# Two layers of a diffusion backbone with an expert layer: the relay of a unit's chosen experts stands later, diagonals three pairs ahead

## The reference, cut to what matters

```python
s1 = jnp.einsum('thd,kd->thk', q1, sub_k1); s2 = jnp.einsum('thd,kd->thk', q2, sub_k2)
v1, i1 = lax.top_k(s1, 16);  v2, i2 = lax.top_k(s2, 16)
cand_s = v1[..., :, None] + v2[..., None, :];  cand_i = i1[..., :, None] * 128 + i2[..., None, :]
best_s, pos = lax.top_k(cand_s, 16);  idx = take_along_axis(cand_i, pos)
gate = softmax(best_s)
act = gelu(einsum('thkd,td->thk', exp_u[idx], hb))
out = einsum('thk,thkd->td', gate * act, exp_v[idx])
```

## Time and profile before

| | us |
|---|---|
| median of 3 runs | 5514.84 (5513.72 to 5514.99) |
| the profiled execution's own time | 5498.03 |
| its span | 5496.2 |
| busy: PE, DVE, POOL, ACT | 4310.1, 3042.9, 2745.0, 1236.3 |
| PE idle for a unit's `gnorm` at its relay | 163.4, 31 times |
| gathers: bytes, mean rate over the span | 1342 MB, 301 GB/s with the weights |

### The profile page before, as it was taken

One profiled execution on the slowest core, in us unless ns is written; L12 is line 12 of the kernel. 1 busy time (PEld: TensorE's weight loads), 2 busy tenths in 40 slices (PEclk: granted clock), 3 DMA queues, 4 the chain that ended last, 5 costly groups with the idle time before them and its releaser, 6 DMA issues.

```text
span 5496.2 us, 57357 instructions
## 1 busy us (share of the span) xinstructions
PE 4310.1 (78%) x19168; PEld 2423.3 (44%) x19168; DVE 3042.9 (55%) x8176; ACT 1236.3 (22%) x3643; POOL 2745.0 (50%) x2566
## 2 busy tenths in 40 slices
PE   7989788888987878997855558999788799655655
PEld 4468643434675345653411115668534455211111
DVE  1211767786227867457677542521687655776753
ACT  1321222333212321122211113530233111111111
POOL 0000566667205655666677770000366566777776
PEclk8789899988998888998977788999888999777788
DMA  5543799999638978999999992114698899999999
GB/s 194 194 172 133 289 368 356 332 341 352 237 134 298 339 283 327 385 396 368 359 386 382 405 387 80 55 62 150 237 330 317 316 358 396 380 397 389 379 409 349
DMA packets 464130, 1651.73 MB, mean 301 GB/s; under 512 B 51168, under 2 KB 57440, under 8 KB 463840
## 3 DMA queue, kind: packets, MB, share of 16 engines
q0 software_dynamic: 368640, 1342.34, 64.3%
q1 hardware_dynamic: 95200, 305.73, 15.5%
HBM read 1645.77 MB, written 2.10 MB: 300 GB/s over the span
## 4 chain that ended last, share of the span: by engine, by line
PE 43%; POOL 20%; DVE 16%; DMA 10%; issue 8%; ACT 3%; SPq 0%; DVEq 0%; POOLq 0%; ACTq 0%; PEldq 0%
PE banks L653 15%; POOL vb L1457 10%; POOL ub L1446 10%; PE banks L934 8%; DMA vb<-in_peer_v_dram,idx 7%; DVE ub L1397 5%; PE banks L742 4%; PE banks L669 3%; PE banks L844 3%; PE banks L821 3%; PE banks L832 1%; PE banks L782 1%; PE banks L721 1%; PE banks L906 1%; DVE region L1257 1%
## 5 line engine op out<-in xcount | busy, mean ns | idle before, releaser
L1446 POOL DMA_INDIRECT ub<-in_peer_u_dram,idx x1280 | 1394.9, 1090 | 2164.8 <-DVE idx L1385 1330.3
L934 PE MATMUL banks<-vb,dg 128*64 128x512 f32 x5120 | 1565.4, 740 | 693.7 <-DMA vb<-in_peer_v_dram,idx 599.8
L1397 DVE CUSTOM_DVE_ANT_0 ub<-ub,h2cur 128x1024 f32<-128x1024 f32 x1280 | 1529.0, 1222 | 591.1 <-DMA ub<-in_peer_u_dram,idx 470.9
L1457 POOL DMA_INDIRECT vb<-in_peer_v_dram,idx x1280 | 1349.5, 1054 | 569.1 <-issue 356.8
L934 PEld LDWEIGHTS banks<-vb,dg 128*64 128x64 f32 x5120 | 407.8, 160 | 1588.0 <-issue 1351.8
L653 PE MATMUL banks<-region,wring 128*128 128x256 f32 x3840 | 885.7, 390 | 39.6 <-ACT region L998 25.3
L653 PEld LDWEIGHTS banks<-region,wring 128*128 128x128 f32 x3840 | 740.1, 195 | 220.8 <-issue 108.3
L1145 ACT ACTIVATE dg<-consts,wgt 128x64 f32<-128x64 f32 x1280 | 358.9, 338 | 829.8 <-PE banks L934 416.9
L653 PE MATMUL banks<-h2T,wring 128*128 128x256 f32 x1280 | 318.1, 406 | 20.8 <-ACT h2T L998 20.8
L1340 DVE SCALAR_TENSOR_TENSOR region<-region,banks 128x256 f32<-128x256 f32 x120 | 50.5, 421 | 488.5 <-PE banks L653 488.4
L742 PE MATMUL banks<-region,wring 128*128 128x256 f32 (+1 forms) x1056 | 260.7, 406 | 48.0 <-ACT region L998 48.0
(11 more groups left out here) (146 smaller groups left out, 3711.4 us busy)
## 6 DMA issues: line engine op xcount, KB each, us to landing
wring<-w_gate_dram SPq DMA_DIRECT2D x120, 512.0 KB, 4.6
wring<-w_mod_dram SPq DMA_DIRECT2D x96, 512.0 KB, 4.5
wring<-w_pq_dram SPq DMA_DIRECT2D x80, 512.0 KB, 6.0
wring<-w_branch_dram SPq DMA_DIRECT2D x60, 512.0 KB, 4.8
wring<-w_out_dram SPq DMA_DIRECT2D x40, 512.0 KB, 4.2
ub<-in_peer_u_dram,idx POOLq DMA_INDIRECT x1280, 6.9
vb<-in_peer_v_dram,idx POOLq DMA_INDIRECT x1280, 6.9
region<-in_na_rpb_dram SPq DMA_DIRECT2D x64, 256.0 KB, 3.1
```

The costliest lines, as they stand in the source:

```text
L934: ins = nc.tensor.matmul(bank(ACC[a])[64 * g:64 * g + 64, :], dg[:, n % DG_RING, :], vb[:, n % V_RING, a * 512:(a + 1) * 512], start=first ...
L1397: nc.vector.tensor_tensor_reduce(out=ub[:, n % U_RING, :], in0=ub[:, n % U_RING, :], in1=h2cur[:, g, :], scale=1.0, scalar=0.0, op0=ALU.mu ...
L1446: pool.indirect_dma_start(ub[:, n % U_RING, :], None, u_rows, bass.IndirectOffsetOnAxis(ap=idx[:, u % IDX_RING, j:j + 1], axis=0)).then_in ...
L1457: pool.indirect_dma_start(vb[:, n % V_RING, :], None, v_rows, bass.IndirectOffsetOnAxis(ap=idx[:, u % IDX_RING, j:j + 1], axis=0)).then_in ...
```

## The change

Relay and index leave the chain of a unit's choice. The choice now has five steps (`topk` 0 to 3 and `gnorm`), and `bgs["front"]` counts five to a unit. The relay of unit `u` is written behind part 1 of unit `u + 1`, its index behind part 3 of `u + 1`, both in the same background step as that part and without a turn of their own. So each background step still has one step of choice (or two), but five instead of seven make a unit. A unit that no later unit's choice follows has its relay and index written by `chosen(u)`, right ahead of its own first dots, or by `until_front` at the start of a query stage. The number of units that the choice may be ahead is as before. Diagonals stand three pairs ahead of the sum instead of two, `wgt` with them one pair earlier. No computation is added or dropped. The foreground, the dots and the sums stand in the same order as before, and so do POOL's and SP's queues.

```diff
-DIAG_LEAD, SUM_LAG = 2, 11
+DIAG_LEAD, SUM_LAG = 3, 11
...
+        def relay_part():
+
+            u, part = divmod(bgs["relayed"], 2)
+            assert not part or bgs["a"] >= PAIRS * (u - IDX_RING + 1)
+            plan.append(("index", u) if part else ("relay", u))
+            bgs["relayed"] += 1
+
         def topk_step():
-            u, part = divmod(bgs["front"], 7)
-            assert part < 6 or bgs["a"] >= PAIRS * (u - IDX_RING + 1)
+
+            u, part = divmod(bgs["front"], 5)
+            plan.append(("topk", u, part) if part < 4 else ("gnorm", u))
             bgs["front"] += 1
-            plan.append(("topk", u, part) if part < 4 else ((("gnorm", u), ("relay", u), ("index", u))[part - 4]))
+            if u and part in (1, 3) and bgs["relayed"] == 2 * (u - 1) + part // 2:
+                relay_part()
+
+        def chosen(u):
+
+            while bgs["front"] < 5 * (u + 1):
+                topk_step()
+            while bgs["relayed"] < 2 * (u + 1):
+                relay_part()
 
         def misc_clear():
 
-            if bgs["front"] % 7 == 6:
-                topk_step()
+            if bgs["relayed"] % 2:
+                relay_part()
...
-                while bgs["front"] < 7 * (u + 1):
-                    topk_step()
+                chosen(u)
...
-                for _ in range(2 if bgs["front"] < 7 * (u + 2) + r else bgs["rate"]):
-                    if bgs["front"] < min(7 * (u + 2 + 8 * bgs["rate"]), 7 * bgs["avail"]):
+                for _ in range(2 if bgs["front"] < 5 * (u + 2) + r else bgs["rate"]):
+                    if bgs["front"] < min(5 * (u + 2 + 8 * bgs["rate"]), 5 * bgs["avail"]):
                         topk_step()
...
-            while bgs["front"] < 7 * PH * (tile + 1):
-                topk_step()
+            chosen(PH * (tile + 1) - 1)
```

More of the change, by code:

```diff
@@ L252, in program @@
         owed = [0.0]
-        bgs = dict(avail=0, front=0, d=0, g=0, a=0, rate=1)
+        bgs = dict(avail=0, front=0, relayed=0, d=0, g=0, a=0, rate=1)
         TILES = [(0, 0), (0, 1), (0, 2), (0, 3), (0, 4), (0, 5), (1, 2), (1, 3), (1, 4), (1, 5)]
+        def relay_part():
[3 more added lines that the diff above has]
+            bgs["relayed"] += 1
         def topk_step():
-            u, part = divmod(bgs["front"], 7)
-            assert part < 6 or bgs["a"] >= PAIRS * (u - IDX_RING + 1)
+            u, part = divmod(bgs["front"], 5)
+            plan.append(("topk", u, part) if part < 4 else ("gnorm", u))
             bgs["front"] += 1
-            plan.append(("topk", u, part) if part < 4 else ((("gnorm", u), ("relay", u), ("index", u))[part - 4]))
+            if u and part in (1, 3) and bgs["relayed"] == 2 * (u - 1) + part // 2:
[5 more added lines that the diff above has]
+                relay_part()
         def misc_clear():
-            if bgs["front"] % 7 == 6:
-                topk_step()
+            if bgs["relayed"] % 2:
+                relay_part()
         def bg_step():
```

## The result

The changed kernel takes **5525.03 us** (median of 21 runs; the kernel before 5514.83 in as many): 1.0021 of the time before, 95% interval 1.0012 to 1.0031. The forecast was 5487. The time lies within the forecast's range, the sign does not: it is 10 us slower, at the edge of what can be measured, where 28 us of gain were expected.

What follows compares the result with a forecast made beforehand. No engine is full, so the limit changes by stretch: DVE, POOL's queue, or PE's relay waits. Gains of 71 less losses of 43 make 28 us off the median 5514.84: 5487, range 5425 to 5538.

Steps and rivals of the forecast that it cites:

- Attention: half of a wait comes back: In attention, half of PE's 44 us of relay waits comes back, 22 us gained; ends 0 and 44.
- rival 3: PE then waits for a V gather or full banks instead; only the merges' later waits go: 5517, chance 0.15.
- rival 2: Denser choice in latent attention and query stages lies on DVE's path, loss 55 instead of 9: slower, 5533, chance 0.20.
- signs of being wrong: A merge keeps 350 us, V gather waits grow as relay waits shrink, or the new POOL waits are absent.
- Merges: most of it comes back: In the two merges, 16 us each of PE's relay waits come back, 32, plus 10 for the clock.
- The choice comes sooner: Nine more top-k parts per latent attention, 19 to 30 us on DVE, a quarter counting: net loss 9; ends 0 and 60.
- Less choice beside the experts alone: Sixteen parts leave the stretches where experts run alone; at 0.48 us a part, gathers gain 7 us, down to 0.
- Three relays come too late: At units 15, 47 and 79 POOL cannot gather ahead: 33 us lost together, ends 20 and 40.
- Query stages: In three query stages DVE sets the end, so nothing changes: zero, -5 to +5 us for each.
- small things: Ten more ScalarE table loads lose 1 us, up to 13; earlier diagonals and DVE's relay waits count 0.
- The clock: Waits that vanish in the merges spare slow-clock PE work: 5 us a merge, 10 for both, ends 0 and 13.
- Rival 1: PE is the limit wherever it waits: all 141 us come back with some 25 of clock: 5383, chance 0.10.

Runs made afterwards that it cites:

- three traces with the order of before: Traces of the kernel before, of it with only units 15, 47 and 79 relayed late (1.0062), and of the probe (1.0040).
- placement kernel: The changed kernel with the choice at seven slots to a unit as before and no late relay at units 15, 47, 79: 0.9942 of the kernel before.
- two kernels of groups two and three with placement at the old pace: The placement kernel (0.9942), and one at seven slots with relay one slot later than before, copy one behind, no late relay (0.9923).
- three dense ones without late relays: The changed kernel without late relays (0.9966), also with second units' relay and copy behind their own choice (0.9963), or relay and copy near their gnorm (0.9987).
- the probe: The kernel before with parts 0, 1 and 3 of the choice done twice for 24 units beside the experts alone: 1.0040.
- five other kernels of groups two and three: Changed kernels without late relays: two at seven slots to a unit (0.9942, 0.9923), three at five slots (0.9963, 0.9987, 0.9966).

## Why the prediction was wrong, point by point

- **"Attention: half of a wait comes back" failed.** This step and the next miss by the same size. 22 us were counted; at the old pace the two latent attentions and tile 1 gave 2.3, 0.6 and 2.2, together 5 (6 to 7 against the three traces with the order of before). One wait was read the earlier trace rows, 3.56 of 7.83 us, and made the price of all. What was not read was the next thing PE needs. In the placement kernel it was V gathers, and 13.0 us at one name became 14.5 us at the other; in the changed kernel it was mostly attention's own values, from a DVE with more choice to do. That was rival 3, "the wait takes another name", which had 0.15. Its 5517 lies 8 us from the measured time, but so does rival 2's 5533, so the number alone decides nothing. Over the span 92 us left the relay and 130 us came to the V gathers, as the prediction had named among its signs of being wrong, though the longer lead of the diagonals has a part in that.
- **"Merges: most of it comes back" held in its place and failed in its size.** 42 us with the clock were forecast; 18.3 and 16.4 came, 35, but of these only part is the waits. With the choice where it was, placement alone gives 11.8 and 13.1, 25 together (placement kernel of the second group; 8 and 13 against the three traces with the order of before). There 22.1 us of relay wait went for 11.8 us of time, so in a merge too a wait was worth about half of itself, in part because 6.3 us came back at the V gathers. In the changed kernel 17.4 us of wait went for 18.3 us of time, but 26 us of DVE's work and 26 of PE's matmuls left that stretch as well. The second half has no relay wait left, as said. The first long wait went from 14.2 to 8.9 us, 5.3 less where 2 had been counted. The 5 us a merge for the clock are not there in the placement kernel: PE's busy time is 303.9 us against 304.5 before for the same matmuls, in layer 1 302.4 against 301.8.
- **"The choice comes sooner" was under-sized.** Nine parts a latent attention were right in size (17.8 us on DVE where 19 to 30 stood), but a quarter of them was said to lie on the path, and it was more. Between the placement kernel (269.6) and the changed one (278.2) lie 8.6 us for 17.8 to 18.0 of DVE, nearly half; in layer 1 9.2 (10.5 and 8.0 with the changed kernel on the same chip). So rival 2's place was right, not its size. Net of what tile 1 and the merges gain, the medians give up to 13 us for 9 forecast and the traces 3; the net is open, as said.
- **"Less choice beside the experts alone" failed.** 7 us of gain were forecast. The two stretches (pairs 284 to 384, and 499 to 632) take 1286.5 and 1290.2 us together in the two kernels of groups two and three with placement at the old pace, and 1288.2, 1286.2 and 1295.6 in the three dense ones without late relays: no gain. The slope of 0.48 us a part came from two windows of the earlier trace rows that differ in more than choice; the probe gives at most 0.30, and the gathers beside the choice's own instructions were not the slow ones. The Trainium skill (SBUF — State Buffer, "SBUF: two separate sides") has it that a DVE instruction with two SBUF inputs and a GpSimd one that reads SBUF shut each other out for a whole instruction. The trace agrees for gathers that start inside a dot product: they last nearly 0.94 us and the rest of it. It shows nothing of the other direction, since a dot product that starts inside a gather keeps its 1.22 us. The probe's dots catch more gathers early (68 of 176 with over 0.4 us left, 53 of 190 before); why they fall that way was not taken apart.
- **"Three relays come too late" was right.** 33 us forecast; 34 measured alone, and 30 from the difference of 1.0021 and 0.9966. The single stalls are 13.5, 9.6 and 8.3 us on POOL, and 10.4 on PE at unit 15, for 11, 11.2 and 11.2 forecast.
- **Query stages, small things: right.** Zero within -5 to +5 was said; 3.0 and 0.6 us are there. The diagonals' lead is worth nothing (0.9992).
- **The clock.** Rival 1, that all of PE's waits come back with their clock, is refuted: 92 us of wait went, and the mean granted clock is 0.868 for 0.869. In the changed kernel's merge it read higher (0.96 for 0.93), of which up to 0.02 is the spread between traces of the same order. The Trainium skill (TensorE: Matmul & The Clock Gate, "HAM oscillation") has it that an idle PE is throttled again at each such gap. That would have given, by the prediction's estimate, some 50 us more, and nothing of the kind was measured.

The sum as measured: placement -32, density +13, late relays +30, lead 0, together +11, where the medians differ by 10. It closes by construction: the terms are the steps between 1, 0.9942, 0.9966 and 1.0021, each from another chip, so that they add up is no check of them. The late relays have one of their own, 34 us measured alone. Forecast were -64 for waits and clock, +2 for the density with the stretches alone, +33 and +1. The miss is 32 us in the first term, about half of it attention (5 for 22) and half the merges with their clock (25 for 42), and up to 11 in the second. These steps turned the sign. The stated range holds the time only because it took in rival 3 and much of rival 2; the mechanism that it gave for attention did not hold.

One more thing was misread, the base: in the profiled execution of before the stretch of pairs 284 to 384 takes 563.4 us, but 565 to 578 in the five other kernels of groups two and three that have no late relay and no doubled parts. The trace of one execution is known to a few us per stretch, no better.

## What to carry to other kernels

A wait is worth what the engine behind it is late by, so ask what it needs next and whether that would be there: read the waits of the same engine on its next inputs before giving any of a wait back. And a step that is tied to the next unit's work needs a rule for the last unit before a pause: here that rule alone, two lines, turned 10 us of loss into 19 us of gain. The least move that frees PE (one slot, at the old pace) did as well as any, 0.9923, within the intervals of the 0.9942 of the larger one.

## What the hardware showed that had not been expected

A gather's issue on POOL takes 0.94 us with DVE idle, hardly more beside the choice (0.98), but a mean of 1.16 beside the dots, which read two tiles of 128x1024. A gather that starts inside a dot product lasts about 0.94 us and the rest of it, up to 1.90 on average; one that is under way when the dot product starts is not lengthened. How busy DVE is tells less than what it runs, and when. And the same kernel took 5514.8 us on one chip and 5805.6 on another, whose mean clock was 0.84 instead of 0.87.
